# Attention in a two-block kernel: probabilities normalised and differenced before they are transposed, values as the weights of the last product

## What is computed

```python
MLA_HEADS = 4     # queries and keys of 96, values of 64
DIFF_HEADS = 4    # two softmaxes each, queries and keys of 32, values of 64
GQA_HEADS = 8     # queries and keys of 64, values of 64, two key heads
...
def _sdpa(q, k, v, scale):
    s = jnp.einsum('bhgqd,bhkd->bhgqk', q, k).astype(jnp.float32) * scale
    p = jax.nn.softmax(s, axis=-1).astype(v.dtype)
    return jnp.einsum('bhgqk,bhkd->bhgqd', p, v)
...
    d = od[:, :, 0] - lam.astype(od.dtype) * od[:, :, 1]     # the two outputs of a differential head
    d = _rms(d, g_diff_sub) * (1.0 - lam_init)
...
y = _merge(o_lat[0], o_lat[1], o_lat[2], lam, lam_init, g_diff_sub[l]) @ w_out[l]
```

## Time and profile before

| | |
|---|---|
| median of three runs | 2812.38 us (2804.35 to 2822.99) |
| the profiled execution | 2807.35 us |
| its span, first to last instruction | 2805.6 us |
| mean granted clock of TensorE | 0.926 |
| TensorE, VectorE, ScalarE busy | 2485.1, 1670.5, 1339.6 us |

### The profile page before, as it was taken

How to read it: one execution, slowest core, us unless ns; L and a number is a source line. 1 busy time by engine, 2 the same in 40 slices (tenths; PEclk the granted TensorE clock), 3 DMA queues, 4 the chain that set the end, 5 groups by cost and what they waited for, 6 DMA issues and landing times.

```text
span 2805.6 us, 40788 instructions
## 1 busy us (share of the span) xinstructions
PE 2485.1 (89%) x16118; PEld 2166.9 (77%) x16118; DVE 1670.5 (60%) x2985; ACT 1339.6 (48%) x2083; POOL 53.4 (2%) x66
## 2 busy tenths in 40 slices
PE   4999989999999999989896799799969987897997
PEld 2877889999866566779795578689959986787897
DVE  4565569889867777654554444554555555443554
ACT  4654444555555555544454343555444443333443
POOL 1000000000000000000000000000000000000000
PEclk8999999999999999989997787899979998777999
DMA  6655546654578778754452101134525552101453
GB/s 216 192 191 164 169 147 201 212 167 145 176 254 262 258 263 265 242 180 161 149 169 75 60 31 46 64 119 150 187 80 181 173 167 85 46 1 61 155 184 128
DMA packets 138125, 433.12 MB, mean 154 GB/s; under 512 B 15377, under 2 KB 38673, under 8 KB 137681
## 3 DMA queue, kind: packets, MB, share of 16 engines
q1 hardware_dynamic: 109424, 396.93, 43.2%
q10 hardware_dynamic: 26208, 23.98, 2.7%
q0 software_dynamic: 2304, 9.60, 1.0%
HBM read 416.56 MB, written 13.89 MB: 153 GB/s over the span
## 4 chain that ended last, share of the span: by engine, by line
PE 63%; DVE 13%; issue 9%; ACT 8%; DMA 4%; POOL 1%; ACTq 0%; POOLq 0%; SPq 0%; DVEq 0%
PE bk L1553 60%; DVE SPL L1001 5%; ACT SPL L669 4%; PE bk L1559 3%; DMA RAW<-in_ada 2%; DVE R L1001 2%; ACT R L671 1%; DVE TMP L1001 1%; POOL ST L578 1%; ACT R L669 1%; DMA kept<-TMP 1%; DVE R L1010 1%; DVE ST L1016 1%; DVE R L1007 1%; DVE HL L1001 1%
## 5 line engine op out<-in xcount | busy, mean ns | idle before, releaser
L1001 DVE TENSOR_TENSOR SPL<-RAW,SPL 128x1024 fp32r<-128x1024 f32 (+1 forms) x758 | 919.5, 1221 | 558.9 <-ACT SPL L669 556.9
L669 ACT ACTIVATE SPL<-RAW 128x1024 fp32r<-128x1024 f32 (+1 forms) x758 | 791.2, 1050 | 398.1 <-PE bk L1553 347.6
L1553 PE MATMUL bk<-HH,SPL 128*128 128x256 f32 x3840 | 751.6, 289 | 19.8 <-DVE R L1001 6.5
L1553 PEld LDWEIGHTS bk<-HH,SPL 128*128 128x128 f32 x3840 | 622.1, 194 | 27.3 <-issue 9.2
L1553 PE MATMUL bk<-SPL,WHL 128*128 128x512 f32 x2328 | 578.8, 398 | 39.5 <-DVE SPL L1001 39.4
L1553 PEld LDWEIGHTS bk<-SPL,WHL 128*128 128x128 f32 x2328 | 430.0, 190 | 156.2 <-issue 70.7
L1553 PE MATMUL bk<-HL,SPL 128*128 128x256 f32 x1920 | 547.4, 285 | 0.0
L1553 PEld LDWEIGHTS bk<-HL,SPL 128*128 128x128 f32 x1920 | 372.9, 194 | 3.1 <-issue 0.7
L1553 PE MATMUL bk<-SPL,HH 128*128 128x256 f32 (+1 forms) x1664 | 317.8, 293 | 22.5 <-DVE HL L1001 13.6
L1553 PE MATMUL bk<-R 128*128 128x64 f32 (+8 forms) x1440 | 312.8, 369 | 25.6 <-ACT R L669 17.2
L669 ACT ACTIVATE R<-bk 128x512 f32<-128x512 f32 (+4 forms) x368 | 180.0, 503 | 275.6 <-PE bk L1553 226.8
(11 more groups left out here) (120 smaller groups left out, 2107.4 us busy)
## 6 DMA issues: line engine op xcount, KB each, us to landing
RAW<-in_peer SPq DMA_DIRECT2D x256, 512.0 KB, 4.8
RAW<-in_ada SPq DMA_DIRECT2D x144, 512.0 KB, 5.1
RAW<-in_ffn SPq DMA_DIRECT2D x132, 512.0 KB, 4.0
RAW<-in_win SPq DMA_DIRECT2D x96, 512.0 KB, 4.3
RAW<-in_ffd SPq DMA_DIRECT2D x66, 512.0 KB, 3.3
RAW<-in_wout SPq DMA_DIRECT2D x32, 512.0 KB, 3.9
kept<-TMP ACTq DMA_DIRECT2D x90, 128.0 KB, 2.8
TMP<-kept ACTq DMA_DIRECT2D x90, 128.0 KB, 4.6
```

The costliest lines, as they stand in the source:

```text
L669: ins = e.activation(out, in_, func, bias=bias, scale=scale)
L1001: e.tensor_tensor(out, a, b, op).then_inc(*dve.up(*points))
L1553: ins = e.matmul(out, lhsT, rhs, start=start, stop=stop, skip_group_check=True)
```

## The change

The order of the 40 units is new: the differential heads first, and for each head its two groups of queries next to each other, the two softmaxes of a differential head innermost.

A new step `nm`, in round n for unit n - 1, divides the probabilities on VectorE in place: a reciprocal of the row sum and a multiplication of 128x512 (128x256 for the context). For the second softmax of a differential head it multiplies the reciprocal by lambda (which the kernel keeps with its sign turned) and adds the first softmax's normalised probabilities, so one matrix is left of two. TensorE's transposes wait for `nm`, and are left out for the first softmax (u = 0): 32 rounds of transposes instead of 40. ScalarE makes all copies of transposes. `PT` becomes two buffers that hold a head's transposed probabilities for all 256 queries.

The last product, `av`, is now made once a head, after its second group of queries. For differential heads the weights are still the transposed probabilities, eight products of 64 columns. For the others the values are the weights (64 columns of them) and the transposed probabilities move, 256 columns: four products a head, and the output comes out already transposed, an even head in partitions 0 to 63 and an odd one in 64 to 127. So a new step `ao` reads each pair of heads from its bank: ScalarE copies the high part, VectorE subtracts for the low part. Only the differential heads' outputs are still transposed (`dT`), after their mean square and scaling for all queries at once (`df_a`, `df_b`, in rounds 20 and 22).

```diff
+def make_units():
+    out = [(1, h, i, u) for h in range(4) for i in range(2) for u in range(2)]
+    return out + [(k, h, i, 1) for k, heads in ((0, 4), (2, 8)) for h in range(heads) for i in range(2)]
...
 def attend_steps(l, s):
     out = []
-    for n in range(43):
-        out += [("as", l, s, n)] * (n < 40) + [("at", l, s, n - 2)] * (2 <= n < 42) + [("av", l, s, n - 3)] * (n >= 3)
-        if n == 24:
-            out += [("aT", l, s, 0, 0), ("aT", l, s, 0, 1)]
-    return out + [("aT", l, s, 1, 0), ("aT", l, s, 1, 1)]
+    for n in range(47):
+        out += [("as", l, s, n)] * (n < 40) + [("nm", l, s, n - 1)] * (1 <= n < 41)
+        if 2 <= n < 42 and UNITS[n - 2][3]:
+            out.append(("at", l, s, n - 2))
+        if 3 <= n < 43 and UNITS[n - 3][2:] == (1, 1):
+            out.append(("av", l, s, head_of(n - 3)))
+        if 5 <= n < 45 and UNITS[n - 5][2:] == (1, 1) and UNITS[n - 5][0] != 1 and UNITS[n - 5][1] % 2:
+            out.append(("ao", l, s, head_of(n - 5) // 2 - 2))
+        out += [("df_a", l, s)] * (n == 20) + [("df_b", l, s)] * (n == 22) + [("dT", l, s)] * (n == 24)
+    return out
...
-COST = {"nT": 0.5, "pj": 5.8, "lr1": 0.6, "lr2": 1.0, "tr": 0.6, "as": 2.0, "at": 0.9, "av": 1.2, "aT": 0.6,
+COST = {"nT": 0.5, "pj": 5.8, "lr1": 0.6, "lr2": 1.0, "tr": 0.6, "as": 1.0, "at": 0.5, "av": 1.5,
...
-    plan += weave(qkv_steps(0, 0, True), attend_steps(0, 1)[:60])
-    plan += weave(attend_steps(0, 0), attend_steps(0, 1)[60:] + out_steps(0, 1) + ffn_steps(0, 1)[:50])
+    plan += weave(qkv_steps(0, 0, True), attend_steps(0, 1)[:70])
+    plan += weave(attend_steps(0, 0), attend_steps(0, 1)[70:] + out_steps(0, 1) + ffn_steps(0, 1)[:50])
...
# VectorE
+            def nm(l, s, n):
+                q, W, (kind, _, _, u) = QS[(l, s)], 256 if s else 512, UNITS[n]
+                r, p = q["RS"][:, n:n + 1], q["PR"][n % 4][:, 0:W]
+                dve.wait_ge(T.at("p", l, s, n))
+                e.reciprocal(r, r).then_inc(*dve.up())
+                if kind == 1 and u == 1:
+                    dve.wait_ge(dve.own, T.at("lam"))
+                    tt(r, r, lamc[:, l:l + 1], ALU.mult)
+                    dve.wait_ge(dve.own)
+                    stt(p, p, r, q["PR"][(n - 1) % 4][:, 0:W], ALU.mult, ALU.add, ("nm", l, s, n))
+                else:
+                    dve.wait_ge(dve.own)
+                    ts(p, p, r, None, ALU.mult, None, ("nm", l, s, n))
...
# TensorE
-                pe.wait_ge(T.at("p", l, s, n))
+                pe.wait_ge(T.at("nm", l, s, n))
...
+                if g < 4:
...
+                            mm(b[:, i * 256 + 64 * g:i * 256 + 64 * g + 64], pt[:, k, i * P:(i + 1) * P], v, k == 0,
+                               k == last, *(done if end else ()))
+                    return
+                key = ("av", l, s, g // 2 - 2)
+                b = ps(*key) if g % 2 else take(key, VALUE[(l, s)])
+                r = slice(64 * (g % 2), 64 * (g % 2) + 64)
+                for k, v in enumerate(vals):
+                    done = [("pv", l, s, g)] + [("full", key)] * (g % 2)
+                    mm(b[r, 0:256], v, pt[:, k, :], k == 0, k == last, *(done if k == last else ()))
```

More of the change, by code:

```diff
@@ L494, in turned_after, with kv_of, score_in, value_in @@
             return T.at({"ka": "ka", "kk": "kk", "pg": "gq"}[n], l, s)
[L496 to L515, removed]
-        def by_act(l, s, n):
-            return n % 2 == 0 or 12 <= n % 20 < 16 or s == 1
+        def kv_of(l, s):
+            return [kv_views(l, 1)] if s else [kv_views(l, 0), kv_views(l, 1)]
+        def score_in(l, s, n):
+            kind, h, i, u = UNITS[n]
+            q, kv, c = QS[(l, s)], kv_of(l, s), slice(i * P, (i + 1) * P)
+            if kind == 0:
+                return q["QM3"][0:96, h, c], [v[0][0:96, h] for v in kv]
+            if kind == 1:
+                d = 2 * h + u
+                r = slice(32 * (d % 4), 32 * (d % 4) + 32)
+                return q["QD3"][r, d // 4, c], [v[1][r, d // 4] for v in kv]
+            r = slice(64 * (h % 2), 64 * (h % 2) + 64)
+            return q["QG3"][r, h // 2, c], [v[2][r, h // 4] for v in kv]
+        def value_in(l, s, g):
+            c = 256 + 64 * g if g < 4 else 64 * (g - 4) if g < 8 else 512 + 64 * ((g - 8) // 4)
+            return [v[3][:, k, c:c + 64] for v in kv_of(l, s) for k in range(2)]
+        def weights_t(l, s, g):
+            nk = 2 if s else 4
+            return QS[(l, s)]["PT"][g % 2][:, 0:256 * nk].rearrange("p (k t) -> p k t", k=nk)
+        def block_of(p):
+            return p if p < 2 else p + 2
         NORM = {
@@ L1827, in as_ @@
                 for m, k in enumerate(ks):
-                    mm(b[:, m * 256:(m + 1) * 256], qa[:, i * P:(i + 1) * P], k, True, True,
-                       *((("full", key),) if m == len(ks) - 1 else ()))
+                    mm(b[:, m * 256:(m + 1) * 256], qa, k, True, True, *((("full", key),) if m == len(ks) - 1 else ()))
             def at(l, s, n):
@@ L1845, in av, with dT @@
                                    T.at("out", ("pj", l, k, 3)))
+                n = max(m for m in range(40) if head_of(m) == g)
                 pe.wait_ge(T.at("out", ("at", l, s, n)))
-                for k in range(nk):
-                    done = [("pv", l, s, n)] + [("full", key)] * final
-                    mm(b[:, 64 * h:64 * h + 64], QS[(l, s)]["PT"][n % 3][:, k * P:(k + 1) * P],
-                       vals[k // 2][:, k % 2, vc:vc + 64], k == 0, k == nk - 1, *(done if k == nk - 1 else ()))
-            def aT_(l, s, i, k):
-                pe.wait_ge(T.at("y", l, s, i))
-                columns(("aT", l, s, i, k), QS[(l, s)]["Y"][:, i * 1024:(i + 1) * 1024], SCORE[(l, s)])
+                if g < 4:
+                    key = ("avd", l, s)
+                    b = take(key, VALUE[(l, s)]) if g == 0 else ps(*key)
+                    for i in range(2):
+                        for k, v in enumerate(vals):
+                            end = i == 1 and k == last
+                            done = [("pv", l, s, g)] + [("full", key)] * (g == 3)
+                            mm(b[:, i * 256 + 64 * g:i * 256 + 64 * g + 64], pt[:, k, i * P:(i + 1) * P], v, k == 0,
[4 more added lines that the diff above has]
+                r = slice(64 * (g % 2), 64 * (g % 2) + 64)
+                for k, v in enumerate(vals):
+                    done = [("pv", l, s, g)] + [("full", key)] * (g % 2)
+                    mm(b[r, 0:256], v, pt[:, k, :], k == 0, k == last, *(done if k == last else ()))
+            def dT(l, s):
+                key, d = ("dT", l, s), QS[(l, s)]["Yd"]
+                b = take(key, SCORE[(l, s)])
+                pe.wait_ge(T.at("yd", l, s))
+                blocks(b, [d[:, i, k * P:(k + 1) * P] for k in range(2) for i in range(2)], P, ("full", key))
             def gB(l, s, k, h):
```

121 lines of the change are left out of this document (54 added, 67 removed).

## The result

The changed kernel takes 2846.19 us (median of 4 runs, 2840.5 to 2847.75) against 2814.73 for the kernel before (4 runs, one more than in the table above): ratio 1.011, 95% interval 1.0073 to 1.0147. It is slower; the forecast was 2795, range 2758 to 2835. The profiled execution's span is 2843.8 us, 38.2 longer than before.

The account below looks back on a forecast made before the run. It took TensorE's work and the clock level it is done at as the bound. The four stretches, +2 - 13 + 4 - 10 = -17 us on a median of 2812.4, gave 2795 us, range 2758 to 2835.

Parts of the forecast that it names:

- C: Stretch where layer 0's latent attention alternates with dense products (1722 to 1926 us): +4 us, between -2 and +12.
- B: Stretch where the context attention's rest alternates with the first latent units only (1633 to 1722 us): -13 us, between 0 and -36.
- A full clock in B: Rival: the context and latent alternation finds full clock, -32 us there, -36 in all, 2776 us; chance 0.18.
- A: Stretch where the context attention begins among layer 0's projections (about 1534 to 1633 us): +2 us, -3 to +8.
- D: Layer 1's latent attention, alone (2409.4 to 2549.9, 140.5 us): sum 130 us, so -10.
- these waits are hidden: Layer 1's latent attention: at half clock TensorE is slower than VectorE's chain, so waits on it add nothing; 3.32 us a unit.
- The waits are not covered: Rival: VectorE's factors delay other work and the single value bank makes TensorE wait: +3 us, 2815; chance 0.18.
- The half clock through D's last units: Rival: a wait drops the clock for layer 1's latent attention's 16 last units: +32 us in all, 2844; chance 0.10.

Follow-up runs that it names:

- e1: Changed kernel without copying out pairs 0 to 4 in layer 0's latent attention, whose value products then never wait for their bank: 2810.23 us.
- e2: Changed kernel with the copy-out of each pair (step ao) one round earlier in the order, complete computation: 2807.62 us, ratio 0.9976 to the kernel before.
- e10: Kernel before with only its unit order changed, all 16 differential units first in each attention; some output transposes moved later: 2875.99 us, ratio 1.0219.
- e4: e2 with the twelve non-differential heads before the four differential ones in layer 0's latent attention: 2784.75 us, ratio 0.9895 to the kernel before.
- e7: e4 with the non-differential heads first in layer 1's latent attention too: 2792.27 us, ratio 0.9945 to the kernel before.
- e9: e4 with layer 1's latent differential scores taken from 96-row operands instead of 32-row ones (result differs): 2766.97 us, ratio 0.9831 to the kernel before.
- e12: e4 with layer 1's latent differential queries zero-padded to 128 rows, same result: 2768.71 us, ratio 0.9836 to the kernel before.
- e8: e4 with two extra, overwritten 96-row score products in each differential unit of layer 1's latent attention: 2816.31 us, ratio 1.0019 to the kernel before.
- e11: e4 with the 64-row scores of layer 1's latent attention made 32-row ones (result differs): 2788.31 us, ratio 0.9898 to the kernel before.
- e6: e2 with two extra, overwritten 96-row score products in each differential unit of layer 0's latent attention: 2815.63 us, ratio 1.0006 to the kernel before.

## Why the prediction was wrong

The step that failed is C's: "+4, between -2 and +12, the latter if the single bank of values, which must be emptied before each next pair of heads, shows", with its price in the rival, "about 0.9 us for each of six pairs". The mechanism was named and mis-sized. 0.9 us is the emptying alone (0.38 + 0.42 here). The wait is that plus what was still ahead of it in the order of two engines, up to 5.8 us, plus the half clock behind it. By e1 and e2 it comes to 33 and 36 us of C. I had read the lag of the emptying as distance in rounds and not compared it with the place of the product that waits, which was in the same round and ahead of it. With the wait gone C is 216.5 us, +12: the upper end that I had allowed for it, where I expected +4. TensorE's idle time is then as it was before (21.4 us for 20.5); what is left is 11.4 us more of busy time for 88 instructions fewer, at a mean clock of 0.92 for 0.95. Why the clock is lower wasn't tried. And "nearly gapless at full clock" was a misreading of the kernel before: of C's 204.2 us TensorE was idle for 20.5.

The second step is B's level: "a mix, nearer the half level" and -13. It was 0.54, and B +2.4. The work was priced well (87 us all at half clock; TensorE was busy for 87.2), the gain from a better level did not come. I knew that the new order leaves only differential units there ("14 latent units, all differential"), and that the clock had fallen in just such units before, but put the product savings and the order into one mix. Taken alone, the order costs the kernel before 61 us, 38 of them in B (e10). In the changed kernel, putting the other heads first in (0,0) is worth 23 (e4 against e2); in (1,0) it is not (e7). A full clock in B was worth -32 in the rival; e4's B is 62.4 us, 27 under the 89.1 before, so it is to be had, though by another order.

The other terms. A: +2 forecast, 0. D: -10 forecast; -16.2 to the first dense product. 2.7 of that is only where D ends: 143.2 has the transposes of the old outputs, which the 140.5 of the forecast leaves out. The sum of D was 130, and 127.0 was measured. The clock's course, "half for all 16", three 96-row units more, then full, is what the windows show, and a pair of 64-row units took 5.27 (5.2 forecast). A group of four differential units at half clock took 13.8 us (2478.75 to 2492.54), 3.45 a unit for 3.32. At half clock "these waits are hidden" was not so: TensorE waited five times for the multiply-add of the second differential unit, 8.9 us in all. The chain's price at full clock, 2.2 a unit, was 2.10 in e9, where it could first be seen. The factor on 128x512 took 487 ns on average, the estimate was 0.48. The four value products took 1.94 where 1.84 was forecast; 12 heads by 0.10 are 1.2 us. The Trainium skill ("TensorEngine Tiling (Array Packing)", Key Properties) has changes of the tiling mode drain the engine; one more a head, at the 0.14 us of the trace before, was to cost 1.7. The trace doesn't contradict it, but doesn't separate a mode change from the product itself.

Rivals. "The waits are not covered" had the right cause at a third of its size (C +12, whole 2815, where the wait alone came to 33 to 36). The half clock through D's last units, which would have given 2844, close to the measured time, did not occur.

Together: -17 forecast and +38.2 measured differ by 55: C 44, B 15, the stretch between C and D 4, A -2, D -6.

## What to carry to other kernels

Where a single buffer passes between engines that work in order, price the wait by the place of the release in each queue relative to the waiter, in the finest order that is issued, not by the duration of the releasing instruction; if the waiter stands ahead of the release in the same round, move the release first. When a change also reorders units, run the old kernel in the new order: here the order alone cost twice as much as the whole change (61 us for 31). And ask at which clock level saved TensorE work would be done; products of a few rows can be made whole-height with zeros at the same number of columns, which was worth 16 us here (e12 against e4) where such products had run at half clock.

## What the runs showed of the hardware

A TensorE that hardly idles can stay at 1.2 GHz: 119.17 us busy of 120 at a granted clock of 0.50 in e10, 64.00 of 64 in e8. And with a fifth of its time idle, in waits of at most 1.3 us, it can hold 2.4 GHz: 25.41 of 32 us in e12. The Trainium skill ("TensorE: Matmul & The Clock Gate", the table of states in Part 1) has a busy array at the full clock and an idle one at half; the rows of e10 and e8 do not fit it, and the measurement decides, while e12's short waits do not speak against it.

What made the difference in (1,0) was that the differential units' score products went from 32 rows to 96 or 128 (e9, e12), even where three quarters of the height are rows of zeros in the weights. Whether it is the height or the change between partial and whole height that goes with it, no run tells. Products added beside the 32-row ones did not do it there (e8: 0.50), and 32-row scores in units with more of other products, entered at full clock, kept it although they have both the low height and the change (e11: 1.00). No single quantity that I tried accounts for all of this; which one the clock follows stays open. The level can also differ between executions of one program: e6 ran in 2782 to 2789 us at a mean clock of 0.93, and in 2813 to 2818 at 0.92.
